# Feed-forward products by seven block products instead of eight, with tokens as the stationary operand

## The chip, the cores and the metric

The kernel runs on one core of one Trainium2 chip. The metric is the time of one execution on the device, in microseconds (us).

## The reference, cut to what matters

Two networks run one after the other on 256 tokens of width 1024: two layers with mixture-of-experts blocks, then two layers that each hold two gated feed-forward blocks of hidden width 2816. All data are float32. Only these four feed-forward blocks change:

```python
def _rmsnorm(x, g):
    xf = x.astype(jnp.float32)
    y = xf * lax.rsqrt(jnp.mean(xf * xf, axis=-1, keepdims=True) + NORM_EPS)
    return (y * g.astype(jnp.float32)).astype(x.dtype)

def _swiglu(x, w_in, w_out):
    gate, up = jnp.split(x @ w_in, 2, axis=-1)
    return (jax.nn.silu(gate) * up) @ w_out
...
        h = h + HALF * _swiglu(_rmsnorm(h, ffn1_norm[l]), ffn1_w_in[l], ffn1_w_out[l])
...
        h = h + HALF * _swiglu(_rmsnorm(h, ffn2_norm[l]), ffn2_w_in[l], ffn2_w_out[l])
```

## The kernel before

Activations lie turned: 128 features in the partitions, 256 tokens along the free dimension, so that the width of 1024 is eight chunks. Weights come by DMA, in tiles of 2 MB (`w_in`) and 1 MB (`w_out`), into a ring of six slots (`SLOTS`). SyncE issues the next tile of one fixed list when a slot comes free (`due`, `follow`, `refill`), always into the slot that was freed first.

`ffn_stage` is one feed-forward block in 11 steps of 256 hidden features. Both products hold a 128x128 piece of a weight as the stationary operand and move the 256 tokens past it. A step is 32 such matmuls for gate and up (`first_hidden` for step 0, L1450; `hidden`, L1465) and 16 for the product with `w_out` (`add`, L1476), which gathers in the four banks 0 to 3 over all steps. VectorE multiplies gate and up by the inverse RMS `r` (L1558, L1559), ScalarE applies silu (L1540), VectorE multiplies the two (L1562). `add` of a step runs on TensorE one step behind `hidden`, which is cover for this chain, except between step 0 and step 1: there `hidden` of step 1 waits for the last multiplication of step 0.

The inverse RMS comes from `vector_sum` (L334 to L336), a matmul with ones (`tensor_mean`, L342, put behind chunk 5 of step 0), `vector_turn` (L348, L349) and `scalar_root` (L355). The stage behind reads the sums out of the banks with `refresh` (L274) and multiplies by a gain with `gained` (L290). Two of the four blocks are `headed`: their input's squares were made in the stage ahead. The other two make them themselves.

In the trace, one float32 matmul of this program shows as two MATMUL and two LDWEIGHTS records; a transpose on TensorE (`pe.transpose`) shows as one of each.

## Time and profile before

| | |
|---|---|
| median of 3 runs | 2952.29 us (2952.22 to 2952.78) |
| the profiled execution: its span | 2949.0 us |
| outside the span, against the median | 3.3 us |
| TensorE busy | 2754.4 us, 93% of the span |
| VectorE busy | 744.4 us, 25% |
| ScalarE busy | 436.3 us, 15% |
| mean granted TensorE clock | 0.991 |
| the four feed-forward blocks, from the first matmul to that of the stage behind | 233.1, 231.5, 232.7 and 231.4 us |

The profile records one execution. The span runs from its first to its last instruction. The four blocks follow one another with a mixer stage between the two of each layer, and every stage waits for the one ahead.

### The profile page before, as it was taken

What the parts mean: (1) busy time and instruction counts of PE and PEld (TensorE: products, weight loads), DVE (VectorE), ACT (ScalarE), POOL (GpSimd) and SP (SyncE); (2) the same over time, 40 slices, a digit from 0 to 9 for tenths busy, and PEclk for the clock granted to TensorE, in tenths of its full rate; (3) what the DMA queues carried; (4) which work ended last, traced back from release to release, by engine and by line L of the source; (5) the groups of instructions that cost most, each with busy time, mean ns of one, the idle gap of its engine ahead of it and who ended that gap; (6) DMA issues with size and microseconds to landing.
All of it is one profiled execution on the core that took longest, in us unless ns stands there. A gap on an engine that the chain in (4) does not pass through costs nothing. (4 is left out here: it accounts for less than half of the span.)

```text
span 2949.0 us, 36516 instructions
## 1 busy us (share of the span) xinstructions
PE 2754.4 (93%) x16086; PEld 1897.0 (64%) x16086; DVE 744.4 (25%) x1552; ACT 436.3 (15%) x896; POOL 0.2 (0%) x4
## 2 busy tenths in 40 slices
PE   7999999888898998878999999999999999999998
PEld 3664433333666332223888888888888888788887
DVE  1242111111232110102111456411121143763111
ACT  2032111111322110001000312000010031221000
POOL 0000000000000000000000000000000000000000
PEclk9999999999999999999999999999999999999999
DMA  8334999999856999999345331234344453302340
GB/s 344 133 158 171 374 428 428 427 428 427 336 228 280 427 428 427 427 428 385 142 159 197 124 143 60 86 130 156 143 150 150 158 181 114 143 31 101 141 158 29
DMA packets 59384, 691.53 MB, mean 234 GB/s; under 512 B 10384, under 2 KB 13072, under 8 KB 14448
## 3 DMA queue, kind: packets, MB, share of 16 engines
q1 hardware_dynamic: 55408, 685.59, 57.9%
q10 hardware_dynamic: 3840, 3.93, 0.4%
q8 instruction: 109, 1.79, 0.3%
q14 instruction: 27, 0.22, 0.0%
HBM read 688.45 MB, written 1.05 MB: 234 GB/s over the span
## 5 line engine op out<-in xcount | busy, mean ns | idle before, releaser
L1465 PE MATMUL banks<-main,weight_ring 128*128 128x256 f32 x2560 | 559.4, 379 | 6.6 <-DVE main L1562 6.6
L1465 PEld LDWEIGHTS banks<-main,weight_ring 128*128 128x128 f32 x2560 | 486.1, 190 | 74.0 <-issue 8.1
L1154 PE MATMUL banks<-weight_ring,main 128*64 128x512 f32 (+1 forms) x1440 | 323.7, 595 | 28.9 <-DMA weight_ring<-in_gate_up 27.9
L1476 PE MATMUL banks<-main,weight_ring 128*128 128x256 f32 x1408 | 310.4, 379 | 0.0
L1476 PEld LDWEIGHTS banks<-main,weight_ring 128*128 128x128 f32 x1408 | 267.5, 190 | 36.4
L1674 PE MATMUL banks<-main,weight_ring 128*128 128x256 f32 x1248 | 275.3, 380 | 0.0
L1674 PEld LDWEIGHTS banks<-main,weight_ring 128*128 128x128 f32 x1248 | 236.5, 190 | 36.0 <-issue 4.5
L1154 PEld LDWEIGHTS banks<-weight_ring,main 128*64 128x64 f32 (+1 forms) x1440 | 90.5, 124 | 229.7 <-issue 182.4
L1558 DVE TENSOR_TENSOR main<-banks,tmp 128x256 f32<-128x256 f32 x88 | 37.3, 424 | 697.8 <-PE banks L1465 695.9
L1179 PE MATMUL banks<-weight_ring,main 128*64 128x512 f32 (+1 forms) x704 | 159.0, 595 | 37.1 <-DMA weight_ring<-in_down 36.7
L1282 DVE TENSOR_TENSOR main<-banks,main 64x512 f32<-64x512 f32 (+1 forms) x64 | 44.3, 692 | 482.5 <-ACT main L1248 482.5
L1540 ACT ACTIVATE main<-main 128x256 f32<-128x256 f32 x88 | 36.6, 416 | 773.5 <-DVE main L1558 773.5
L1179 PEld LDWEIGHTS banks<-weight_ring,main 128*64 128x64 f32 (+1 forms) x704 | 44.7, 124 | 148.9 <-issue 101.3
L1154 PE MATMUL banks<-main 128*32 128x512 f32 (+1 forms) x384 | 87.0, 595 | 10.3 <-DMA main<-in_gate_up 8.7
L1287 DVE COPY main<-banks 32x512 f32<-32x512 f32 x48 | 33.1, 690 | 244.7 <-PE banks L1179 244.2
L428 PE MATMUL banks<-main,weight_ring 128*128 128x512 f32 (+1 forms) x224 | 82.6, 527 | 6.3 <-ACT main L584 6.3
L1248 ACT ACTIVATE main<-banks 64x512 f32<-64x512 f32 (+1 forms) x64 | 37.5, 586 | 236.9 <-PE banks L1154 236.9
L428 PEld LDWEIGHTS banks<-main,weight_ring 128*128 128x128 f32 x224 | 44.2, 201 | 42.8 <-issue 36.9
L1893 DVE TENSOR_TENSOR main<-banks,tmp 128x256 f32<-128x256 f32 x86 | 35.7, 421 | 133.6 <-PE banks L1674 132.9
L1253 ACT ACTIVATE main<-banks 32x512 f32<-32x512 f32 x48 | 28.1, 586 | 266.1 <-PE banks L1179 265.8
L1450 PE MATMUL banks<-main,weight_ring 128*128 128x256 f32 x256 | 58.5, 388 | 7.4 <-DVE main L290 3.7
L1154 PEld LDWEIGHTS banks<-main 128*32 128x32 f32 (+1 forms) x384 | 22.9, 118 | 64.9 <-issue 49.3
(403 smaller groups left out, 2667.0 us busy)
## 6 DMA issues: line engine op xcount, KB each, us to landing
weight_ring<-in_gate_up SPq DMA_DIRECT2D x90, 2048.0 KB, 34.7
weight_ring<-in_f_in SPq DMA_DIRECT2D x44, 2048.0 KB, 7.7
weight_ring<-in_down SPq DMA_DIRECT2D x43, 2048.0 KB, 35.4
main<-in_gate_up SPq DMA_DIRECT2D x24, 2048.0 KB, 33.7
weight_ring<-in_mix_in SPq DMA_DIRECT2D x24, 2048.0 KB, 7.7
weight_ring<-in_ada_w SPq DMA_DIRECT2D x22, 2048.0 KB, 16.4
weight_ring<-in_f_out SPq DMA_DIRECT2D x44, 1024.0 KB, 4.8
constants<-in_gate_up SPq DMA_DIRECT2D x14, 2048.0 KB, 32.6
```

The costliest lines, as they stand in the source:

```text
L428: return pe.matmul(K.PS[:, c % BANKS, 0:m_], w[:, k, col * P:(col + 1) * P], H[:, k, 0:m_], start=k == 0, stop=k == KC - 1)
L1154: m = pe.matmul(K.PS[64 * j:64 * j + S * CAP, hf, :], x, w[:, k, j, :], start=kh + k == 0, stop=4 * kh + k == KC - 1, tile_position=(0, 64 ...
L1179: m = pe.matmul(K.PS[64 * j:64 * j + S * CAP, 3 + j, :], hT[:, k, 0:S * CAP], w[:, k % 4, j, :], start=k == 0, stop=k == KC - 1, tile_posi ...
L1248: K.mark(a_.activation(hs[64:64 + S * CAP, hf, :], K.PS[0:S * CAP, hf, :], ACT.Silu), K.act)
L1282: K.mark(v.tensor_tensor(hs[64:64 + S * CAP, hf, :], K.PS[64:64 + S * CAP, hf, :], hs[64:64 + S * CAP, hf, :], ALU.mult), K.dve)
L1450: m = pe.matmul(K.PS[:, 4 + c, g * SEQ:(g + 1) * SEQ], w[:, k, g, c * P:(c + 1) * P], H[:, k, :], start=g + k == 0, stop=g == 1 and k == K ...
L1465: m = pe.matmul(K.PS[:, 4 + c, g * SEQ:(g + 1) * SEQ], w[:, k, g, c * P:(c + 1) * P], H[:, k, :], start=g + k == 0, stop=g == 1 and k == K ...
L1476: m = pe.matmul(K.PS[:, o // 2, (o % 2) * SEQ:(o % 2 + 1) * SEQ], w[:, c, o * P:(o + 1) * P], hid[:, b, c, :], start=first and c == 0 and ...
L1540: a_.activation(sg[:, c, :], sg[:, c, :], ACT.Silu).then_inc(K.act.h, 1)
L1558: v.tensor_tensor(sg[:, c, :], K.PS[:, 4 + c, 0:SEQ], N.r, ALU.mult).then_inc(K.linear.h, 1)
L1674: m = pe.matmul(K.PS[:, bank(p), 0:SEQ], wt[:, k, (p % 4) * P:(p % 4 + 1) * P], H[:, k, :], start=k == 0, stop=k == KC - 1)
L1893: K.mark(v.tensor_tensor(Z[:, chunk, :], K.PS[:, bank(p), 0:SEQ], N.r, ALU.mult), K.read)
```

## The change

Gate and up. The normed tokens are made once (`Hn`, with `r` in them) and cut into a 2x2 grid: two halves of the 256 tokens (`t0`, `t1`) by two halves of the 1024 features. A weight tile is cut the same way, two halves of the features by two halves of its columns, each half holding 128 gate and 128 up columns (`ffn_tiles` lays it out so). Strassen's scheme (in Winograd's form) makes the four output blocks from seven block products in place of eight. Sums of token blocks (`S`) are made once per stage, differences of weight blocks (`mingle`) for every tile. In each block product the 128 tokens are stationary and 256 weight columns move, so the outputs come with tokens in the partitions. Step 0 stays as it was.

ScalarE copies four partial sums out of the banks in each step, VectorE adds three (`join`, `finish`), and both make the hidden values (`low`). These are turned back by four transposes a step (`turn`) and kept for all steps (`hid`).

The product with `w_out` now comes behind all gate products, no longer between them, again as seven products per 256 hidden features, each of them one matmul that moves 512 columns, summed over the 11 steps in seven banks. VectorE combines the banks, and 16 transposes turn the result (`turn_out`). The list of weight tiles follows the new order. `tensor_mean` stands behind chunk 2 (`headed`) or chunk 4. The loops are written out; before, they were hardware loops.

The diff, cut to its core (the old body of `ffn_stage`, which it removes, stands above):

```diff
         if self.source == "products":
-            p = K.PS[:, c // 2, (c % 2) * SEQ:(c % 2 + 1) * SEQ]
+            p = K.PS[:, 2 * (c // 4):2 * (c // 4) + 2, (c % 4) * P:(c % 4 + 1) * P]
+            x = x.rearrange("p (i t) -> p i t", i=TT)
...
-    MEAN = 6
+    n1 = n0 + STEPS
+    MEAN, TURNED, SIDE, OTHER = 6, 0, 2, 7
+    MEAN_AT = 2 if headed else 4
...
+            def product(out, a, t, b, begin, end):
+                for k in range(4):
+                    m = pe.matmul(out, a[:, k, t], b[:, k, :], start=begin and k == 0, stop=end and k == 3, skip_group_check=True)
+                return m
+            def turn(j):
+                pe.wait_ge(K.dve.h, hidden(j, 2))
+                if j > 1:
+                    pe.wait_ge(K.hread.h, K.hread.at(j - 1))
+                for place, i in enumerate((0, 2, 3, 1)):
+                    m = pe.transpose(K.PS[:, TURNED, place * P:(place + 1) * P], low[:, j % 2, i, :], K.ident)
+                K.mark(m, K.hturned)
+            def step(j):
+                n = n0 + j
+                b11, b12, b21, b22 = blocks(n)
+                T = B.T[:, j % 2]
...
+                if j == 1:
+                    pe.wait_ge(K.smade.h, K.smade.at(2))
+                if j > 2:
+                    pe.wait_ge(K.dve.h, hidden(j - 2, 2))
+                K.mark(product(main(j), Hn[:, 0:4], t0, b11, True, False), K.formed)
+                pe.wait_ge(K.mingled.h, weighed(n, 1))
+                if j == 1:
+                    pe.wait_ge(K.smade.h, K.smade.at(3))
+                else:
+                    pe.wait_ge(K.joined.h, joined(j - 1, 3))
+                K.mark(product(other(j), S[:, 2], t0, T[:, 0], True, False), K.formed)
+                if j > 1:
+                    turn(j - 1)
+                pe.wait_ge(K.mingled.h, weighed(n, 3))
+                if j == 1:
+                    pe.wait_ge(K.smade.h, K.smade.at(6))
+                pe.wait_ge(K.copied.h, copied(j, 1))
+                K.mark(product(main(j), S[:, 1], t0, T[:, 1], False, False), K.formed)
+                K.mark(product(side(j), Hn[:, 4:KC], t0, b21, True, True), K.formed)
+                pe.wait_ge(K.copied.h, copied(j, 3))
+                K.mark(product(main(j), S[:, 0], t0, b12, False, False), K.formed)
+                pe.wait_ge(K.mingled.h, weighed(n, 4))
+                K.mark(product(other(j), Hn[:, 4:KC], t1, T[:, 2], False, True), K.formed)
+                pe.wait_ge(K.copied.h, copied(j, 4))
+                K.mark(product(main(j), S[:, 3], t0, b22, False, True), K.used)
+            def add(u, i):
+                b11, b12, b21, b22 = rows(u)
+                T, n = B.TO[:, u % 3], n1 + u
+                if i == M1:
+                    K.arrived(pe, n)
...
+                    a, b = hid[:, 2 * u, t0], b11
+                elif i == M2:
+                    a, b = hid[:, 2 * u + 1, t0], b21
+                elif i == M6:
+                    pe.wait_ge(K.mingled.h, weighed(n, 4))
...
+                    a, b = sums(u, 1), T[:, 1, :]
...
+                    a, b = sums(u, 2), T[:, 0, :]
+                elif i == M4:
+                    a, b = hid[:, 2 * u + 1, t1], T[:, 2, :]
...
+                    a, b = sums(u, 0), b12
+                else:
+                    a, b = sums(u, 3), b22
+                return pe.matmul(K.PS[:, BANK[i], :], a, b, start=u == 0, stop=u == STEPS - 1, skip_group_check=True)
+            def turn_out(i, bank):
+                pe.wait_ge(K.banked.h, K.banked.at(i))
+                for c in range(4):
+                    m = pe.transpose(K.PS[:, bank, c * P:(c + 1) * P], ends[:, 2 + i, c * P:(c + 1) * P], K.ident)
+                K.mark(m, K.turned_out)
+            first_hidden()
+            for j in range(1, STEPS):
+                step(j)
+            for u in range(LATE):
+                for i in (M1, M2, M6, M7, M4, M5, M3):
+                    m = add(u, i)
+                K.mark(m, K.used)
+                if u == 0:
+                    turn(STEPS - 1)
+            for i in (M1, M2, M6, M7, M4, M5, M3):
+                for u in range(LATE, STEPS):
+                    m = add(u, i)
+                if i != M3:
+                    K.mark(m, K.summed_out)
+                if i == M7:
+                    pe.wait_ge(K.hread.h, K.hread.at(STEPS - 1))
+                    turn_out(1, 0)
+                if i == M5:
+                    turn_out(2, 1)
+            m.then_inc(K.used.h, 3)
+            K.used.count += 3
+            turn_out(3, 3)
+            turn_out(4, 2)
...
+            for j in range(1, STEPS):
+                if j > 1:
+                    a_.wait_ge(K.joined.h, joined(j - 1, 2))
+                copy(j, m1s, main(j), M1)
+                copy(j, m7s, other(j), M7)
+                if j > 1:
+                    a_.wait_ge(K.joined.h, joined(j - 1, 3))
+                copy(j, qs, main(j), M6)
+                if j > 1:
+                    read_turned(j - 1)
+                copy(j, q5s, main(j), M5)
+                if j == 1:
+                    for c in range(2):
+                        a_.wait_ge(K.linear.h, K.linear.at(2 * c + 1))
+                        K.mark(a_.activation(B.sg0[:, c, :], B.sg0[:, c, :], ACT.Silu), K.act)
+                a_.wait_ge(K.joined.h, joined(j, 3))
+                if j > 1:
+                    a_.wait_ge(K.dve.h, hidden(j - 1, 1))
+                K.mark(a_.activation(B.sg[:, 0:3, :], B.cs[:, :, t0], ACT.Silu), K.act)
+                a_.wait_ge(K.used.h, n0 + j + 1)
+                if j > 1:
+                    a_.wait_ge(K.dve.h, hidden(j - 1, 2))
+                K.mark(a_.activation(B.sg[:, 3, :], main(j)[:, t0], ACT.Silu), K.act)
...
+            def mingle_begin(n, parts, T):
+                b11, b12, b21, b22 = parts
+                K.arrived(v, n)
+                difference(T[:, 0], b22, b12)
+                difference(b12, b12, b11)
+            def mingle_end(n, parts, T):
+                b11, b12, b21, b22 = parts
+                settle()
+                difference(T[:, 1], b22, b12)
+                settle()
+                difference(T[:, 2], b21, T[:, 1])
...
+            def mingle(j):
+                parts = blocks(n0 + j), B.T[:, j % 2]
+                if j > 2:
+                    v.wait_ge(K.used.h, n0 + j - 1)
+                mingle_begin(n0 + j, *parts)
+                mingle_end(n0 + j, *parts)
...
+            def mingle_out(u):
+                parts = rows(u), B.TO[:, u % 3]
+                if u > 2:
+                    v.wait_ge(K.used.h, n1 + u - 2)
+                mingle_begin(n1 + u, *parts)
+                mingle_end(n1 + u, *parts)
...
+            def share(part, a, b):
+                pair = hid[:, 2 * a:2 * b, :].rearrange("p (u c) t -> p u c t", c=2)
+                a11, a12, a21, a22 = pair[:, :, 0, t0], pair[:, :, 1, t0], pair[:, :, 0, t1], pair[:, :, 1, t1]
+                out = B.shares[part]
+                K.mark(v.tensor_tensor(out[:, 0], a21, a22, ALU.add), K.shared)
+                K.mark(v.tensor_tensor(out[:, 2], a11, a21, ALU.subtract), K.shared)
+                v.wait_ge(K.shared.h, K.shared.at(4 * part + 1))
+                K.mark(v.tensor_tensor(out[:, 1], out[:, 0], a11, ALU.subtract), K.shared)
+                v.wait_ge(K.shared.h, K.shared.at(4 * part + 3))
+                K.mark(v.tensor_tensor(out[:, 3], a12, out[:, 1], ALU.subtract), K.shared)
...
+            def join(j):
+                v.wait_ge(K.formed.h, formed(j, M2))
+                v.wait_ge(K.copied.h, copied(j, 1))
+                if j > 1:
+                    v.wait_ge(K.dve.h, hidden(j - 1, 1))
+                K.mark(v.tensor_tensor(B.cs[:, 0, :], m1s, side(j), ALU.add), K.joined)
+            def finish(j):
+                v.wait_ge(K.copied.h, copied(j, 4))
+                K.mark(v.tensor_tensor(B.cs[:, 1, :], q5s, m7s, ALU.add), K.joined)
+                v.wait_ge(K.formed.h, formed(j, M4))
+                K.mark(v.tensor_tensor(B.cs[:, 2, :], qs, other(j), ALU.add), K.joined)
+                v.wait_ge(K.act.h, K.act.at(2 + 2 * (j - 1) + 1))
+                if j > 2:
+                    v.wait_ge(K.hturned.h, K.hturned.at(j - 2))
+                v.wait_ge(K.joined.h, joined(j, 3))
+                K.mark(v.tensor_tensor(low[:, j % 2, 0:3, :], B.cs[:, :, t1], B.sg[:, 0:3, :], ALU.mult), K.dve)
+                v.wait_ge(K.act.h, K.act.at(2 + 2 * (j - 1) + 2))
+                v.wait_ge(K.used.h, n0 + j + 1)
+                K.mark(v.tensor_tensor(low[:, j % 2, 3, :], main(j)[:, t1], B.sg[:, 3, :], ALU.mult), K.dve)
...
+            for b in range(2):
+                K.mark(v.tensor_tensor(Hn[:, 4 * b:4 * b + 4, :], H[:, 4 * b:4 * b + 4, :], bc(N.r, 1, 4), ALU.mult), K.smade)
+            v.wait_ge(K.smade.h, K.smade.at(2))
+            K.mark(v.tensor_tensor(S[:, 2], Hn[:, 0:4, t0], Hn[:, 0:4, t1], ALU.subtract), K.smade)
+            K.mark(v.tensor_tensor(S[:, 0], Hn[:, 0:4, t1], Hn[:, 4:KC, t1], ALU.add), K.smade)
+            v.wait_ge(K.smade.h, K.smade.at(4))
+            K.mark(v.tensor_tensor(S[:, 1], S[:, 0], Hn[:, 0:4, t0], ALU.subtract), K.smade)
+            v.wait_ge(K.smade.h, K.smade.at(5))
+            K.mark(v.tensor_tensor(S[:, 3], Hn[:, 4:KC, t0], S[:, 1], ALU.subtract), K.smade)
+            mingle_end(n0 + 1, *first)
+            gate_begin()
+            for j in range(1, STEPS):
+                if j > 1 and j + 1 < STEPS:
+                    mingle(j + 1)
+                if j == STEPS - 1:
+                    mingle_out(0)
+                    v.wait_ge(K.used.h, n0 + STEPS - 1)
+                    share(0, 0, 5)
+                join(j)
+                if j == 1:
+                    mingle(2)
+                    gate_end()
+                finish(j)
+            mingle_out(1)
+            v.wait_ge(K.used.h, n0 + STEPS)
+            v.wait_ge(K.hread.h, K.hread.at(STEPS - 1))
+            share(1, 5, STEPS)
+            for u in range(2, STEPS):
+                mingle_out(u)
+            m1, q, u3, c11, c21, c22, c12 = (ends[:, i, :] for i in range(7))
+            v.wait_ge(K.copied.h, K.copied.at(4 * (STEPS - 1) + 1))
+            v.wait_ge(K.summed_out.h, K.summed_out.at(2))
+            combine(c11, m1, K.PS[:, BANK[M2], :], K.banked)
+            v.wait_ge(K.summed_out.h, K.summed_out.at(3))
+            st(v.tensor_tensor(q, m1, K.PS[:, BANK[M6], :], ALU.add))
+            v.wait_ge(K.summed_out.h, K.summed_out.at(4))
+            st(v.tensor_tensor(u3, q, K.PS[:, BANK[M7], :], ALU.add))
+            v.wait_ge(K.summed_out.h, K.summed_out.at(5))
+            combine(c21, u3, K.PS[:, BANK[M4], :], K.banked)
+            v.wait_ge(K.summed_out.h, K.summed_out.at(6))
+            st(v.tensor_tensor(q, q, K.PS[:, BANK[M5], :], ALU.add))
+            combine(c22, u3, K.PS[:, BANK[M5], :], K.banked)
+            v.wait_ge(K.turned_out.h, K.turned_out.at(2))
+            following.vector_early(v)
+            v.wait_ge(K.used.h, n1 + STEPS)
+            combine(c12, q, K.PS[:, BANK[M3], :], K.banked)
+            if gains:
+                if loads:
+                    K.all_loaded(v)
+                following.vector_gained(v)
+            v.wait_ge(K.turned_out.h, K.turned_out.at(4))
...
-            for j in range(1, FC // 2):
-                t += [(TILE, win[layer, j]), (2 * D, wout[layer, j - 1])]
-            return t + [(2 * D, wout[layer, FC // 2 - 1])]
+            return [(TILE, win[layer, j]) for j in range(FC // 2)] + [(2 * D, wout[layer, j]) for j in range(FC // 2)]
```

## Rows read from the trace of the kernel before

**Rows 1.** Part 1 of the page: busy time and share of the engines.

```profile
PE 2754.4 (93%) x16086; PEld 1897.0 (64%) x16086; DVE 744.4 (25%) x1552; ACT 436.3 (15%) x896; POOL 0.2 (0%) x4
```

**Rows 2.** Busy time by stretch: the four blocks. Columns: stretch, length, engines, clock, DMA.

```profile
1382.90:1616.00 233.10, 230.50 (x1058) 202.01 (x1059) 33.85 (x84) 12.95 (x29) 0.00 (x0) 0.99 0.45 168
...
1923.80:2155.30 231.50, 228.84 (x1059) 200.90 (x1059) 32.28 (x77) 12.33 (x26) 0.00 (x0) 1.00 0.41 149
2155.30:2388.00 232.70, 230.10 (x1064) 202.00 (x1065) 36.65 (x92) 16.30 (x38) 0.00 (x0) 1.00 0.44 159
...
2704.70:2936.10 231.40, 228.78 (x1058) 200.78 (x1058) 31.96 (x76) 12.51 (x27) 0.00 (x0) 1.00 0.31 113
```

**Rows 3.** The same view: one step of the first block.

```profile
1435.32:1456.04 20.72, 20.72 (x98) 18.24 (x97) 2.36 (x6) 0.83 (x2) 0.00 (x0) 1.00 0.42 153
```

**Rows 4.** Timeline, start of the first block: start, length, engine and instruction, idle time before.

```profile
1382.89 12.29 PE L1450 MATMUL banks<-main,weight_ring 128*128 128x256 f32 x48 [3.68 <-DVE main L290]
...
1384.49 1.22 DVE L334 TENSOR_TENSOR main<-main 128x1024 f32<-128x1024 f32 x1
...
1395.01 0.59 PE L342 MATMUL banks<-tmp,constants 128*128 128x256 f32 x2
...
1395.44 3.62 PE L1450 MATMUL banks<-main,weight_ring 128*128 128x256 f32 x16
1395.64 0.42 DVE L348 TENSOR_SCALAR tmp<-banks 128x256 f32<-128x256 f32 x1 [8.74 <-PE banks L342]
...
1398.34 0.42 DVE L1558 TENSOR_TENSOR main<-banks,tmp 128x256 f32<-128x256 f32 x1 [0.48 <-ACT tmp L355]
...
1400.13 0.43 DVE L1562 TENSOR_TENSOR main<-main 128x256 f32<-128x256 f32 x1 [1.04 <-ACT main L1540]
...
1400.71 14.05 PE L1465 MATMUL banks<-main,weight_ring 128*128 128x256 f32 x64 [1.65 <-DVE main L1562]
```

**Rows 5.** Timeline of TensorE in the mixer: eight transposes (L1709) between matmuls.

```profile
1678.78 1.89 PE L1674 MATMUL banks<-main,weight_ring 128*128 128x256 f32 x8
1680.51 1.04 PE L1709 MATMUL banks<-constants,main 128*128 128x128 f32 x8
1681.38 0.81 PE L1674 MATMUL banks<-main,weight_ring 128*128 128x256 f32 x3
```

**Rows 6.** Groups by line: transposes of another stage. Busy us, mean ns of one.

```profile
L2151 PE MATMUL banks<-constants,main 128*128 128x128 f32 x64 | 8.2, 277 | 2.1 <-PEq L1628 2.1
```

**Rows 7.** Timeline of TensorE in the first network: matmuls that move 512 columns.

```profile
217.69 7.13 PE L962 MATMUL banks<-main,constants 128*128 128x512 f32 x16
224.66 0.60 PE L944 MATMUL banks<-constants,main 128*128 128x128 f32 x4
225.10 7.03 PE L962 MATMUL banks<-main,constants 128*128 128x512 f32 x16
231.97 0.60 PE L944 MATMUL banks<-constants,main 128*128 128x128 f32 x4
```

**Rows 8.** Groups by line, shapes apart: VectorE and ScalarE pieces of the size used.

```profile
L334 DVE TENSOR_TENSOR main<-main 128x1024 f32<-128x1024 f32 x6 | 7.3, 1224 | 1.1 <-PEq L2019 1.1
...
L858 ACT ACTIVATE main<-banks 128x512 f32<-128x512 f32 x16 | 9.6, 597 | 9.6 <-PE banks L759 9.5
...
L1540 ACT ACT_TABLE_LOAD x4 | 5.1, 1283 | 0.1
...
L858 ACT ACTIVATE main<-banks 128x256 f32<-128x256 f32 x8 | 3.1, 383 | 7.1 <-PE banks L759 7.1
```

**Rows 9.** Timeline of TensorE at the first block's end; L1662 is the mixer's.

```profile
1601.08 13.98 PE L1476 MATMUL banks<-main,weight_ring 128*128 128x256 f32 x64
1616.01 1.32 PE L1662 MATMUL banks<-main,weight_ring 128*128 128x256 f32 x5 [0.95 <-PEq L1440]
```

**Rows 10.** DMA issues of weights: KB each, median us from issue to landing.

```profile
weight_ring<-in_f_in SPq DMA_DIRECT2D x44, 2048.0 KB, 7.7
...
weight_ring<-in_f_out SPq DMA_DIRECT2D x44, 1024.0 KB, 4.8
```

More of the change, by code:

```diff
@@ L1425, with ffn_stage @@
 EXP_M_HALF = float(np.exp(-0.5))
[L1428 removed]
+def ffn_stage(K, N, B, headed, following, gains, loads=()):
     nc, n0, STEPS, H = K.nc, K.eaten, FC // 2, N.H
[L1433 to L1481 removed]
@@ new lines, in ffn_stage, with blocks @@
+    n1 = n0 + STEPS
+    MEAN, TURNED, SIDE, OTHER = 6, 0, 2, 7
+    MEAN_AT = 2 if headed else 4
+    M1, M7, M6, M2, M5, M4, M3 = range(7)
+    BANK = {M1: 4, M2: 5, M6: 6, M7: 7, M4: 1, M5: 3, M3: 2}
+    LATE = STEPS - 3
+    Hn, S, hid, low, ends = B.Hn, B.S, B.hid, B.low, B.ends
+    t0, t1 = slice(0, P), slice(P, 2 * P)
+    m1s, m7s, qs, q5s = (B.mid[:, i, :] for i in range(4))
+    def blocks(n):
+        w = K.slot(n).rearrange("p (k h f) -> p k h f", k=KC, h=2)
+        return w[:, 0:4, 0, :], w[:, 0:4, 1, :], w[:, 4:KC, 0, :], w[:, 4:KC, 1, :]
@@ new lines, in rows, with sums, main, other @@
+    def rows(u):
+        w = K.slot(n1 + u)[:, 0:2 * D].rearrange("p (c f) -> p c f", c=2)
+        return w[:, 0, 0:512], w[:, 0, 512:1024], w[:, 1, 0:512], w[:, 1, 512:1024]
+    def sums(u, i):
+        return B.shares[0][:, i, u, :] if u < 5 else B.shares[1][:, i, u - 5, :]
+    def main(j):
+        return K.PS[:, 1 if j % 2 else 3, 0:SEQ]
+    def other(j):
+        return K.PS[:, OTHER, 0:SEQ]
+    def side(j):
+        return K.PS[:, SIDE, 0:SEQ]
+    def formed(j, product):
+        return K.formed.at(6 * (j - 1) + product + 1)
@@ L1537, in silu, with first_hidden @@
-        def silu(a_, j):
-            for c in range(2):
-                a_.wait_ge(K.linear.h, 2 * j + K.linear.at(c + 1))
-                a_.activation(sg[:, c, :], sg[:, c, :], ACT.Silu).then_inc(K.act.h, 1)
+            def first_hidden():
+                K.arrived(pe, n0)
+                w = K.slot(n0).rearrange("p (k h g f) -> p k h g f", k=KC, h=2, g=2)
+                for k in range(KC):
+                    if not headed:
+                        pe.wait_ge(K.scaled.h, N.scaled_at(k))
+                    for c in range(2):
+                        for g in range(2):
+                            m = pe.matmul(K.PS[:, 4 + c, g * SEQ:(g + 1) * SEQ], w[:, k, c, g, :], H[:, k, :],
+                                          start=g + k == 0, stop=g == 1 and k == KC - 1, skip_group_check=True)
+                        if k == KC - 1:
+                            K.mark(m, K.used if c == 1 else K.pe)
+                    if k == MEAN_AT:
+                        N.tensor_mean(pe, MEAN)
@@ new lines, in gate_begin, with gate_end @@
+            def gate_begin():
+                for c in range(2):
+                    if c == 0:
+                        v.wait_ge(K.pe.h, K.pe.at(1))
+                    else:
+                        v.wait_ge(K.used.h, n0 + 1)
+                    K.mark(v.tensor_tensor(B.sg0[:, c, :], K.PS[:, 4 + c, 0:SEQ], N.r, ALU.mult), K.linear)
+                    K.mark(v.tensor_tensor(B.up0[:, c, :], K.PS[:, 4 + c, SEQ:2 * SEQ], N.r, ALU.mult), K.linear)
+            def gate_end():
+                for c in range(2):
+                    v.wait_ge(K.act.h, K.act.at(c + 1))
+                    v.wait_ge(K.linear.h, K.linear.at(2 * c + 2))
+                    K.mark(v.tensor_tensor(hid[:, c, :], B.up0[:, c, :], B.sg0[:, c, :], ALU.mult), K.dve)
@@ L1569, in _ @@
             N.vector_sum(v, st, here=not headed)
+            first = blocks(n0 + 1), B.T[:, 1]
+            mingle_begin(n0 + 1, *first)
             N.vector_turn(v, st, MEAN)
             N.ready(v)
-            gate(v, 0, 0)
-            gate(v, 1, 1)
-            with v.Fori(0, LOOPS) as i:
-                for b in range(BODY):
-                    gate(v, BODY * i + b + 2, (b + 2) % 3)
-            if loads:
-                K.all_loaded(v)
-            following.vector_early(v, gains)
-    K.pe.count += 2 * STEPS
```

198 lines of the change are left out of this document (73 added, 125 removed).

## The prediction

> **What bounds the kernel now.** I read the page's busy shares first: TensorE has 93% of the span, VectorE 25%, ScalarE 15% [rows 1]. Then the busy time by stretch, for the four feed-forward blocks: in 233.1 us TensorE is busy for 230.5, and the others look the same, at a granted clock of 0.99 to 1.00 and with the DMA engines at 0.31 to 0.45 [rows 2]. So TensorE's own pace sets these blocks. One step of 48 matmuls takes 20.72 us with TensorE busy throughout [rows 3]: 0.4317 us per float32 matmul of 256 columns. The weight loads are busy for 18.24 of the 20.72 us and lie beside the matmuls, so only moved columns count. VectorE works 2.36 us of a step. Last, the timeline: TensorE idles 1.65 us ahead of step 1, for the chain inverse RMS, silu, product [rows 4], and 0.95 us between two stages [rows 9].
>
> **Removed: matmuls.** Gate and up keep 32 matmuls in step 0 and go from 32 to 28 in each of 10 steps, all of 256 columns: 40 x 0.4317 = 17.3 us per block. The product with `w_out` goes from 176 matmuls of 256 columns (76.0 us) to 77 of 512. In the first network, eight of 512 columns take 224.66 - 217.69 = 6.97 us, and another eight 6.87 [rows 7]: 0.871 and 0.859 us each, against 0.863 for twice a 256-column one. I take 0.863, hence 66.5 us, 9.5 less; the two ends are 67.1 and 66.1.
>
> **Added on TensorE: transposes.** 4 for each of 10 steps and 16 at the end, 56 per block. Eight of them in the midst of matmuls like these take 1681.38 - 1680.51 = 0.87 us, and four take 225.10 - 224.66 = 0.44 [rows 5, 7], so 0.11 each: 6.2 us per block.  The other end is the recorded length of one, 0.277 [rows 6], if each had to wait for the one ahead; the rows show starts 0.11 apart, so I take 0.11.
> The Trainium skill ("TensorE: Matmul & The Clock Gate", Part 4: PE-mode transpose) puts a 128x128 transpose in a kernel's midst at about 275 ns. As a length that agrees with the 277 here. Were it the pace too, the four blocks would pay 61.6 us instead of 24.6; the starts in this trace speak against it.
>
> Steady work: 17.3 + 9.5 - 6.2 = 20.6 us less per block, 82.4 in all four.
>
> **A gate step in its new form.** TensorE needs 28 x 0.4317 + 0.44 = 12.5 us, seven products of 1.73. What it must wait for, with releases by [rows 4]: from a matmul to VectorE 0.2 us after TensorE's next instruction starts (1395.44 to 1395.64; I allow 0.3); from the end of a VectorE piece to TensorE 0.15 (1400.56 to 1400.71). A ScalarE copy of 256 columns is 0.38 us [rows 8]. So a copy's round trip is about 0.3 + 0.38 + 0.15 = 0.8 us. Each of the three that TensorE waits for (ahead of M6, M5 and M3) has one whole product of another bank as its cover, 1.73 us. `read_turned` (0.60) comes ahead of the copy behind M5, but is done by then: it starts after M6's copy and M2 and M5 run beside it. The sum `qs + other`, for which the next step's M7 waits, is made after M4 and has M3 and M1 as cover, 3.5 us. `turn` waits for silu and two products of the step before: ready about 1.2 us into the step, needed at 3.5. Were that cover gone, each copy would cost its round trip, 0.8 us.
> VectorE: four differences of 1024 elements at 1.22 [rows 8], three sums of 256 at 0.42, products of 384 and 128 (0.56 and 0.29, from 1.22 and 0.42 by 1.04 ns per element): 7.0 us of 12.5. It runs `mingle` from 1.2 to 6.2 us of the step and `join` is due at 7.6. ScalarE: four copies, one read of 0.60, silu of 384 and 128: 3.0 us, and two table loads of 1.28 [rows 8] at most if silu and copy should not share a table, which would lie where ScalarE waits.
>
> **Start of a block.** Now 1.65 us is lost ahead of step 1. `tensor_mean` moves up. In a `headed` block it is put behind 3 chunks, 5.2 us in, and r is ready 3.3 us later (1395.01 to 1398.34 in [rows 4]), at 8.5. Then VectorE makes `Hn` (two of 1.22), `S` (four of 0.69), two weight differences (1.22): the first product can start at 11.2, M6 at 15.3; TensorE comes at 14.3 and 17.7. No loss. (The first block's first 24 matmuls took 12.1 us, 1382.89 to 1395.01, where 24 x 0.4317 is 10.4, at a lower granted clock; step 0 stays, and so does that.) In the other two the mean is at 8.6, r at 12.0, `Hn` at 14.5, the third sum that M6 needs at 18.8 where TensorE comes at 18.0: 1.0 lost with the first wait. In all four, VectorE does `gate_begin`, `join`, `mingle(2)` (4.9) and `gate_end` in step 1, and its last sum is late for step 2's M7 by about 0.5. Against 4 x 1.65 = 6.6 lost now, that makes 2 x 1.0 + 4 x 0.5 = 4.0: 2.6 us less. What is late next is this VectorE queue in step 1.
>
> **From gate to output.** VectorE can make `share(1)` only when the last step is turned and read: 7.4 us into the output part, then 3.9 for it and 2.9 for `mingle_out(2)`, 14.2, where M6 of u = 2 comes at 14.25. I charge 0.15 per block, 0.6.
>
> **End of a block.** After M3, `c12` (0.69) waits until VectorE is through with four `refresh`; then `turn_out(4)`. From M3's end to the last transpose some 1.6 us, 0.9 of it counted as transposes above: 0.7 more per block, 2.8. The 0.95 between stages [rows 9] stays. The last stage has one `refresh` less to do, 0.4 back.
>
> **DMA.** A gate step asks for 2 MB in 12.5 us and an output step for 1 MB in 6.0; they land in 7.7 and 4.8 us, six slots ahead [rows 10]. The last three slots come free together at a block's end, but the mixer needs the fourth tile some 40 us later. SyncE's queue holds nothing else. I charge nothing.
>
> **Sum.** 82.4 + 2.6 - 0.6 - 2.8 + 0.4 = 82.0 us. The profiled span of 2949.0 becomes 2867.0; 3.3 us lie between it and the median of the runs, so 2870.3: **2870 us**.
>
> **Rivals.**
> 1. The seven products don't run through: one release per gate step is exposed, a copy's full round trip of 0.8 us in each of 40 steps, 32 us, 2902. For it: seven handovers a step where there were two, and three engines in one ring. Against: every cover above is at least twice its wait. 8%.
> 2. Transposes cost their length: 224 x (0.277 - 0.11) = 37 us, 2907. For it the length in [rows 6], against it the starts in [rows 5, 7]. 4%.
> 3. VectorE becomes the bound, and the kernel slower. From 7.0 us of work per step it would have to reach 12.5 to cost anything and 14.6 to eat the 82 us (2.05 us in each of 40 steps), from where on it is slower; at 15 us per step, 2970. The mechanism would be that pieces which read weights from the ring slow down beside TensorE and the DMA. Against: L334 took 1.22 us beside matmuls, the same as its mean [rows 4, 8]. 3%.
> That the kernel would not do what the change says I see no way for.
>
> **Range and chances.** The forecast has 83%. Its own range: low, 0.859 per 512 columns and the start and end losses gone, 2863; high, 0.871 to 0.88 (5 us), transposes at 0.13 (4 us), start and end losses doubled (7 us), 2886. The 80% range reaches somewhat into rival 1: 2862 to 2888. Beyond the low end 2% remain. Faster or slower by 0.2% (5.9 us) is about what a measurement of this kernel can tell from no change; rivals 1 and 2 are still faster, so faster 96%, same 1%, slower 3%.
>
> **What would show it.** Gate steps of 12.5 us with TensorE busy throughout and copies ended before their product's turn; an output step of 6.0; transposes 0.11 apart; blocks of some 211 us in place of 231 to 233, VectorE busy for more than half of each. Wrong if gate steps are longer than 13 us, if the profile names ScalarE or VectorE ahead of M6, M5 or M3, or if 512 columns cost more than 0.88.

## The result, and the profile after

The changed kernel takes 2865.6 us (median of 4 runs, 2862.0 to 2870.2), beside 2952.5 us for the kernel before (4 runs, 2952.2 to 2952.9): a ratio of 0.9703, with a 95% interval of 0.9692 to 0.9715, or 86.9 us less. Forecast were 2870 us and 82.0 us less.

The page of the changed kernel, part 1, answers to [rows 1]:

```profile
PE 2677.1 (93%) x15198; PEld 1711.8 (60%) x15198; DVE 1102.0 (38%) x1932; ACT 517.5 (18%) x1100; POOL 0.2 (0%) x4
```

TensorE keeps its share of 93%, now of a shorter span. It works 77 us less than before, VectorE 358 us more and ScalarE 81 us more, and nearly all of that extra work is hidden (the block starts below show what is not). The four blocks, cut from the first matmul of each to that of the stage behind (busy time by stretch, as [rows 2]):

```profile
1387.57:1598.99 211.42, 210.06 (x836) 154.66 (x837) 123.47 (x180) 33.26 (x80) 0.00 (x0) 0.99 0.45 167
1906.58:2115.62 209.04, 207.87 (x837) 153.64 (x837) 121.87 (x173) 32.58 (x77) 0.00 (x0) 1.00 0.40 147
2115.62:2325.35 209.73, 208.37 (x836) 153.47 (x837) 124.68 (x183) 35.20 (x85) 0.00 (x0) 1.00 0.45 166
2646.26:2855.52 209.26, 207.87 (x836) 153.61 (x836) 121.70 (x172) 32.86 (x78) 0.00 (x0) 1.00 0.31 115
```

They sum to 839.45 us. Before, cut in the same way, it was 233.12 + 231.43 + 231.43 + 231.47 = 927.45 us (the third stretch of [rows 2] reaches 1.3 us into the stage behind). So the blocks give 88.0 us. The rest of the program, which the change leaves alone, took 7.3 us more in this one profiled execution (2868.3 - 839.45 = 2028.85 against 2949.0 - 927.45 = 2021.55). Over the profiled executions of all kernels in this study it lies anywhere between 2021.5 and 2029.9, whatever was edited. Two stretches of the first network, before it reaches any changed code, show what differs. First the kernel before, then the changed one (75 to 100 and 150 to 175 us):

```profile
75.00:100.00 25.00, 25.00 (x119) 19.41 (x118) 2.63 (x5) 2.48 (x4) 0.00 (x0) 0.95 0.38 163
150.00:175.00 25.00, 24.28 (x148) 14.46 (x149) 11.65 (x32) 14.57 (x27) 0.00 (x0) 1.00 0.98 418
```

```profile
75.00:100.00 25.00, 25.00 (x111) 19.71 (x110) 2.66 (x5) 2.48 (x4) 0.00 (x0) 0.89 0.40 170
150.00:175.00 25.00, 24.10 (x141) 14.22 (x141) 10.85 (x30) 12.50 (x23) 0.00 (x0) 0.93 1.01 430
```

The third column from the end is the granted clock: 0.89 for 0.95 and 0.93 for 1.00, in code that is the same. The profiled execution was also the longest of the four. Hence the experiments below are read by the sum of the four blocks. Where an edit touches nothing, blocks 2 to 4 repeat to 0.01 us (the change against diff4late, below). Block 1 has one more source of change: its first 20 matmuls took 10.4 us in most profiled executions, at the lower clock for a part of them, and 8.7 us at full clock in exposed, diff4 and early. Those three sums are 1.7 us shorter for a reason that is not their edit.

One steady gate step (busy time by stretch, beside [rows 3]), then the joint between two steps in TensorE's timeline:

```profile
1457.46:1469.99 12.53, 12.53 (x62) 11.04 (x61) 6.84 (x10) 2.82 (x7) 0.00 (x0) 1.00 0.46 176
```

```profile
1430.68 1.89 PE L1515 MATMUL banks<-main,constants 128*128 128x256 f32 x8
...
1432.40 0.60 PE L1524 MATMUL banks<-constants,main 128*128 128x128 f32 x4
...
1432.84 0.38 PE L1515 MATMUL banks<-main,constants 128*128 128x256 f32 x1
```

A step lasts 12.53 us and TensorE is busy throughout, VectorE for 6.84 and ScalarE for 2.82 of it, where 12.5, 7.0 and 3.0 were forecast. Four transposes (L1524) take 1432.84 - 1432.40 = 0.44 us. The `w_in` and `w_out` tiles land 7.7 and 4.8 us after their issue, as in [rows 10].

The start of step 1 in the first block answers to [rows 4], the end of the block to [rows 9]. The timeline, all engines:

```profile
1401.29 2.36 DVE L1769 TENSOR_TENSOR main<-main,tmp 128x1024 f32<-128x1024 f32 x2 [0.48 <-ACT tmp L362]
...
1403.80 1.97 PE L1515 MATMUL banks<-weight_ring,main 128*128 128x256 f32 x8
...
1405.60 4.02 PE L1515 MATMUL banks<-main,constants 128*128 128x256 f32 x16
...
1407.61 1.23 DVE L1670 TENSOR_TENSOR main<-weight_ring,main 128x1024 f32<-128x1024 f32 x1
1407.62 1.59 PEld L1515 LDWEIGHTS banks<-main,constants 128*128 128x128 f32 x8 [0.54 <-DVE main L1670]
...
1417.52 0.41 DVE L1731 TENSOR_TENSOR constants<-constants,banks 128x256 f32<-128x256 f32 x1
...
1418.09 1.95 PE L1515 MATMUL banks<-main,constants 128*128 128x256 f32 x8
...
1596.57 0.60 PE L1593 MATMUL banks<-constants 128*128 128x128 f32 x4
1597.58 0.66 PE L1593 MATMUL banks<-constants 128*128 128x128 f32 x4 [0.41 <-DVE constants L1759]
1598.99 1.32 PE L1894 MATMUL banks<-main,weight_ring 128*128 128x256 f32 x5 [0.76 <-PEq L1488]
```

`Hn` (L1769) is ready 0.2 us after TensorE could have used it: the 12 matmuls from 1398.40 on end by their pace at 1403.58, and M1 starts at 1403.80. M7 and M6 of step 1 take 1409.45 - 1405.60 = 3.85 us where two products take 3.45: 0.4 us go where M6 waits for a weight difference (L1670). M7 of step 2 (1418.09) starts 0.16 us after the end of VectorE's last sum (L1731, 1417.93). The last four transposes wait 0.41 us for `c12` (L1759), and 0.76 us lie before the next stage.

What the start of a block costs is best read from a block's first matmul to a point where TensorE runs through again, less the matmuls between at 0.4317 us each. An idle time in the profile is shorter than this loss, since it counts from the modelled end of the last matmul, 0.16 us behind its place by the pace (a product of four matmuls shows 1.89 us, and the next starts 1.73 after it). Block 3 of the kernel before, then blocks 2 (`headed`) and 3 of the changed one, timeline of TensorE:

```profile
2155.28 10.60 PE L1450 MATMUL banks<-main,weight_ring 128*128 128x256 f32 x48 [0.95 <-PEq L1440]
...
2185.30 7.07 PE L1476 MATMUL banks<-main,weight_ring 128*128 128x256 f32 x32
```

```profile
1906.58 5.42 PE L1505 MATMUL banks<-main,weight_ring 128*128 128x256 f32 x24 [1.38 <-PEq L2251]
...
1936.50 0.60 PE L1524 MATMUL banks<-constants,main 128*128 128x128 f32 x4
...
2115.62 8.87 PE L1505 MATMUL banks<-main,weight_ring 128*128 128x256 f32 x40 [0.76 <-PEq L1488]
...
2146.24 0.60 PE L1524 MATMUL banks<-constants,main 128*128 128x128 f32 x4
```

Before, 65 matmuls, the mean's among them (28.06 us), take 30.02: 1.96 us lost. Now 69 matmuls (29.79 us) take 29.92 in block 2 and 30.62 in block 3: 0.13 and 0.83 us lost. The other two blocks agree, block 1 without the 1.7 us of lower clock that it has in both kernels.

### The profile page after: what moved, and what is told of

Its sections match the earlier page's. It is cut to its first block and busy times, and to the rows that moved or that the text cites. A ratio compares the mean times of both kernels' runs of the same rounds, so it can differ in the third digit from the quotient of the medians.

```text
span 2868.3 us, 35136 instructions
## 1 busy us (share of the span) xinstructions
PE 2677.1 (93%) x15198; PEld 1711.8 (60%) x15198; DVE 1102.0 (38%) x1932; ACT 517.5 (18%) x1100; POOL 0.2 (0%) x4
## 5 line engine op out<-in xcount | busy, mean ns | idle before, releaser
L1906 PE MATMUL banks<-main,weight_ring 128*128 128x256 f32 x1248 | 275.9, 381 | 0.0
L1906 PEld LDWEIGHTS banks<-main,weight_ring 128*128 128x128 f32 x1248 | 236.9, 191 | 36.1 <-issue 4.4
L1670 DVE TENSOR_TENSOR main<-weight_ring 128x1024 f32<-128x1024 f32 (+1 forms) x168 | 158.3, 942 | 67.0 <-PE banks L1587 64.2
L1587 PE MATMUL banks<-weight_ring,main 128*128 128x512 f32 x352 | 158.9, 592 | 0.0
L1515 PE MATMUL banks<-main,constants 128*128 128x256 f32 x640 | 151.4, 380 | 0.3
L1515 PE MATMUL banks<-weight_ring,main 128*128 128x256 f32 x640 | 151.3, 379 | 0.1
L1515 PE MATMUL banks<-weight_ring,constants 128*128 128x256 f32 x640 | 151.2, 379 | 0.0
L1515 PEld LDWEIGHTS banks<-weight_ring,main 128*128 128x128 f32 x640 | 121.4, 190 | 17.3 <-issue 0.9
L1515 PEld LDWEIGHTS banks<-weight_ring,constants 128*128 128x128 f32 x640 | 121.6, 190 | 16.5
L1515 PEld LDWEIGHTS banks<-main,constants 128*128 128x128 f32 x640 | 118.3, 190 | 16.2 <-DVE main L1670 1.1
L1587 PE MATMUL banks<-main 128*128 128x512 f32 x264 | 119.8, 592 | 0.0
L1587 PEld LDWEIGHTS banks<-weight_ring,main 128*128 128x128 f32 x352 | 66.3, 190 | 78.7 <-issue 78.4
L1161 PE MATMUL banks<-main 128*32 128x512 f32 (+1 forms) x384 | 86.9, 595 | 9.5 <-DMA main<-in_gate_up 7.9
```

The costliest lines, as they stand in the source:

```text
L1161: m = pe.matmul(K.PS[64 * j:64 * j + S * CAP, hf, :], x, w[:, k, j, :], start=kh + k == 0, stop=4 * kh + k == KC - 1, tile_position=(0, 64 ...
L1515: m = pe.matmul(out, a[:, k, t], b[:, k, :], start=begin and k == 0, stop=end and k == 3, skip_group_check=True)
L1587: return pe.matmul(K.PS[:, BANK[i], :], a, b, start=u == 0, stop=u == STEPS - 1, skip_group_check=True)
L1670: K.mark(v.tensor_tensor(out, a, b, ALU.subtract), K.mingled)
L1906: m = pe.matmul(K.PS[:, bank(p), 0:SEQ], wt[:, k, (p % 4) * P:(p % 4 + 1) * P], H[:, k, :], start=k == 0, stop=k == KC - 1)
```

## The experiments

Ten kernels ran. All but turns2, diff4, diff8 and diff4late do only work that the result needs; those four do some of it twice or more often, and nothing was left out of any. "Blocks" is the sum of the four block lengths in the profiled execution.

| kernel | time, us | blocks, us | against the change's 839.45 |
|---|---|---|---|
| before | 2952.5 | 927.45 | +88.0 |
| change | 2865.6 | 839.45 | |
| both8 | 2971.2 (4 runs) | 945.24 | +105.8 |
| gate8 | 2939.1 (1) | 907.49 | +68.0 |
| out8 | 2901.0 (1) | 877.21 | +37.8 |
| exposed | 2906.1 (1) | 878.10 | +38.7 |
| turns2 | 2893.9 (1) | 862.17 | +22.7 |
| mean5 | 2878.9 (1) | 847.76 | +8.3 |
| diff4 | 2893.1 (1) | 866.40 | +27.0 |
| diff8 | 3067.9 (1) | 1038.51 | +199.1 |
| early | 2868.9 (5) | 837.55 | -1.9 |
| diff4late | 2868.7 (4) | 839.48 | +0.0 |

**1. Eight products for seven: both8, gate8, out8.** The orientation, the order and the transposes stay as in the change; both parts, the gate products alone, or the output alone are made of eight plain block products, without weight differences, sums of token blocks and ScalarE's copies of partial sums; VectorE copies the finished banks.

```diff
-                K.mark(product(main(j), Hn[:, 0:4], t0, b11, True, False), K.formed)
...
-                K.mark(product(main(j), S[:, 3], t0, b22, False, True), K.used)
+                product(side(j), Hn[:, 0:4], t0, b11, True, False)
+                K.mark(product(side(j), Hn[:, 4:KC], t0, b21, False, True), K.formed)
...
+                product(main(j), Hn[:, 0:4], t0, b12, True, False)
+                K.mark(product(main(j), Hn[:, 4:KC], t0, b22, False, True), K.used)
```

> The new orientation alone: tokens stationary, weights moving, the same transposes and the same order of tiles, but eight block products in place of seven, in the gate steps 1 to 10 and in the output; no sums of tokens, no differences of weights, no partial sums (VectorE copies the finished banks). Theory (TensorE's moved columns set the blocks, all else is covered): 4 x 10 x 4 x 0.4317 = 69.1 us for the gate products and 4 x 11 x 0.859 = 37.8 for the output, less 1 to 2 us at the starts, over the changed kernel's 2865.6: 2971, so slower than the kernel before by some 19 us; blocks of about 235.5 us. Rival (part of the gain is the orientation, 512-column matmuls and fewer weight loads): no slower than 2952.

> Only the gate steps by eight products, tokens stationary, without weight differences, token sums and ScalarE copies; the output stays at seven. Theory: 69 us more, less about 1 us at the starts: blocks of 209.3 + 17 = 226.5 us, the whole 2934. Rival (the work that the seven products put on VectorE and ScalarE costs TensorE time): taking it away gives some back, blocks clearly under 225 us.

> Only the output by eight products of 512 columns, without differences, sums of hidden values and combined banks; the gate steps stay at seven. Theory: 11 matmuls of 0.859 us more per block, 9.4, less 0.2 where VectorE's queue at the seam is gone: blocks of 218.5 us, the whole 2903. Rival (covers at the seam or at the end cost more than seen): under 217 us.

both8 took 2971.2 us (2970.0 to 2973.5), a ratio to the kernel before of 1.0056 with an interval of 1.0039 to 1.0073: what the change brings beside the seventh product (the orientation with its transposes, the later output, the earlier mean) makes the kernel slower by 17.8 us in the blocks, or 0.6%. The 224 transposes at 0.11 us, 24.4 us, are more than all of it; the gains at the start and from 512 columns give a part back. One of its gate steps, by stretch:

```profile
1450.33:1464.58 14.25, 14.25 (x69) 12.55 (x68) 2.12 (x5) 1.40 (x3) 0.00 (x0) 1.00 0.40 147
```

14.25 us with TensorE busy throughout, against 12.52 or 12.53: the eighth product is 1.73 us, four matmuls of 0.4317. VectorE has 2.12 us of work here and 6.84 in the seven-product step, and TensorE's time differs by the product alone. Gate and output add up without remainder: 68.0 + 37.8 = 105.8. The output's 37.8 is 11 matmuls of 0.859 us in four blocks, to the tenth. The gate's 68.0 stands against 40 x 1.727 = 69.1: about 1.1 us is what the extra waits of the seven-product form cost in all, nearly all of it in blocks 1 and 3.

**2. One release exposed in each gate step: exposed.** M6 is issued ahead of M7, so that it no longer has a product between itself and the copy of M1 for which it waits.

```diff
-    M1, M7, M6, M2, M5, M4, M3 = range(7)
+    M1, M6, M7, M2, M5, M4, M3 = range(7)
```

> M6 straight behind M1 on the same bank, so that ScalarE's copy of M1 between them has no product as its cover; M7 and the transposes come behind M6, everything else as in the changed kernel. Theory: the round trip of release, copy and release shows in every gate step, 0.8 us x 40 = 32 us: steps of 13.3 us, the whole 2898. Rival (the copies are not on the path even so, since TensorE runs ahead through its queue): no change, steps of 12.5.

Two steps' joint in the timeline of TensorE:

```profile
1428.21 1.89 PE L1515 MATMUL banks<-weight_ring,main 128*128 128x256 f32 x8
1430.72 3.69 PE L1515 MATMUL banks<-main,constants 128*128 128x256 f32 x16 [0.63 <-ACT constants L1626]
1434.25 0.60 PE L1524 MATMUL banks<-constants,main 128*128 128x128 f32 x4
...
1441.60 1.89 PE L1515 MATMUL banks<-weight_ring,main 128*128 128x256 f32 x8
1444.11 3.69 PE L1515 MATMUL banks<-main,constants 128*128 128x256 f32 x16 [0.63 <-ACT constants L1626]
1447.64 0.60 PE L1524 MATMUL banks<-constants,main 128*128 128x128 f32 x4
```

M1 starts at 1428.21 and M6 at 1430.72, 2.51 us later where a product takes 1.73: 0.78 us of idle, the round trip that the prediction had put together from single releases as 0.8. The step is 1447.64 - 1434.25 = 13.39 us, 0.87 longer, since the two products behind the wait take 0.08 more as well. That is 35 us in 40 steps, where 32 were expected, and blocks 2 and 4 are 8.7 us longer each, ten times this. Blocks 1 and 3 have 2.6 and 2.9 us more, in step 1, where M6 now comes earlier than VectorE's differences: a wait of 1.86 us in each, and in block 1 a granted clock of 0.67 over the 5.24 us behind it. (The sum of 38.7 holds the 1.7 us by which the first matmuls of block 1 were faster here.) The cover is real: rival 1 describes the price rightly, and the order M1, M7, M6 is what avoids it.

**3. Every transpose twice: turns2.**

```diff
-                for place, i in enumerate((0, 2, 3, 1)):
+                for place, i in 2 * list(enumerate((0, 2, 3, 1))):
...
-                for c in range(4):
+                for c in 2 * list(range(4)):
```

> All transposes of hidden values and of the output are made twice into the same place, 224 more in all. Theory (they cost the distance of their starts, 0.11 us): 24.6 us more, 6.2 per block. Rival (they cost their recorded length of 0.273): 61 us more, 15.3 per block.

```profile
1430.78 1.89 PE L1515 MATMUL banks<-main,constants 128*128 128x256 f32 x8
1432.50 1.04 PE L1524 MATMUL banks<-constants,main 128*128 128x128 f32 x8
1433.38 1.89 PE L1515 MATMUL banks<-main,constants 128*128 128x256 f32 x8
```

224 more transposes cost 22.7 us, 0.10 each; eight of them take 1433.38 - 1432.50 = 0.88 us. At 0.109 each they would be 24.4; at each block's end the four that are added ahead of the last four fall into the wait for `c12`, which is gone from the list of waits here. In the changed kernel the recorded length of one is 273 ns on average (160 on L1524), so length and pace differ by a factor of 2.5, and rival 2 is out. The 275 ns that the Trainium skill ("TensorE: Matmul & The Clock Gate", Part 4: PE-mode transpose) gives for a transpose in a kernel's context, in a passage on bf16, agree with the length of these float32 ones and are not their price.

**4. A later mean: mean5.** `tensor_mean` stands behind chunk 5, as before the change.

```diff
-    MEAN_AT = 2 if headed else 4
+    MEAN_AT = 5
```

> The matmul of the mean square goes back behind chunk 5 of step 0, where it was before. Theory: the inverse RMS comes at 13.7 us, the first block product at 16.3 in place of 14.3, and M6 waits 0.6 more: 2.6 us lost ahead of M6 in each block against 0.2 (headed) and 0.6 (the others): 2.4 and 2.0 more per block, 8.8 in all. Rival (the first product only waits for the weights): no change.

TensorE waits 1.79 us for `Hn` (`PE banks L1515 <- DVE main L1769`, 7.1 us in 4 waits), and the blocks take 8.3 us more. Without the moved mean the change would have lost at a block's start what the kernel before lost there.

**5. VectorE loaded: diff4 and diff8.** In every `mingle` of a gate step, the last weight difference is made five or nine times in place of once, which adds 4 or 8 operations of 1.25 us.

```diff
-                difference(T[:, 2], b21, T[:, 1])
+                for _ in range(extra):
+                    difference(T[:, 2], b21, T[:, 1])
+                    settle()
+                difference(T[:, 2], b21, T[:, 1])
```

> The last weight difference of each gate tile from the second on is made five times over (the same values), 4 x 1.22 us more VectorE work in 9 gate steps of each block: 7.0 + 4.9 + settling = 12.1 us of the 12.52 that TensorE needs. Theory (covered as long as VectorE's step is shorter than TensorE's): 0 to 4 us more in all. Rival (every microsecond of VectorE work costs): 36 x 4.9 = 176 us more.

> The same with 8 more differences, 9.8 us more per gate step: VectorE needs about 17.0 us in a step. Theory: VectorE is now the bound and the step becomes its sum, 17.0 to 17.5 us in place of 12.52, 36 x 4.5 to 5.0 = 162 to 180 us more, 3028 to 3046; that is where the change would have been slower than the kernel before. Rival (something else is hidden in the step): steps well away from VectorE's sum.

diff8 was expected slower than the kernel before, and was: 3067.9 us. A step lasts 17.21 us and VectorE sets it. Busy time by stretch:

```profile
1478.57:1495.78 17.21, 14.44 (x60) 12.22 (x60) 16.27 (x19) 2.60 (x7) 0.00 (x0) 0.90 0.37 146
```

So the bound of rival 3 exists and lies where it was put: a gate step on VectorE that is longer than TensorE's 12.5 us. But the blocks' 199 us are more than the expected 162 to 180, and diff4, expected at 0 to 4 us, lost 27.0. The waits of TensorE in diff4 name the place:

```profile
PE banks L1518 <- DVE constants L1737: 19.5, 4, 4.9
```

and the timeline of TensorE and VectorE in its first block the time:

```profile
1409.98 6.27 DVE L1673 TENSOR_TENSOR main<-weight_ring,main 128x1024 f32<-128x1024 f32 x5
...
1417.17 0.41 DVE L1737 TENSOR_TENSOR constants<-constants,banks 128x256 f32<-128x256 f32 x1
...
1417.73 3.75 PE L1518 MATMUL banks<-main,constants 128*128 128x256 f32 x8 [4.86 <-DVE constants L1737]
1421.28 1.06 PE L1527 MATMUL banks<-constants,main 128*128 128x128 f32 x4
1422.13 2.28 PE L1518 MATMUL banks<-main,constants 128*128 128x256 f32 x8
```

Four waits of 4.9 us, one per block, all at M7 of step 2: in step 1 VectorE has `gate_begin` and `gate_end` beside the usual work, and five microseconds of added differences turn into 4.86 of waiting at once. By starts M7 comes 5.02 us late (1417.73 against 1410.98 + 1.73) for 5.0 us of added work, so nothing was free there. Behind the wait the clock is down: the product takes 3.55 us (1421.28 - 1417.73) at a granted clock of 0.50, the lower of the two levels, and the next is mixed (0.71 over the 9 us from 1417.73; the expectation for diff4late below says 0.67). That makes the wait cost 6.6 to 7.7 us per block, 28.7 in all, and the 27.0 are these less the 1.7 of block 1's faster first matmuls. It explains diff8 too: one first wait of 9.9 us per block, and eight later steps that are 4.7 us longer each (17.21 - 12.52), make 47.4 per block, and the clock behind the first wait the 2.4 that are left to 49.8.

**6. The same load, but not in step 1: diff4late.** To see whether that one place made all of diff4's loss, the four added differences begin in step 2.

```diff
-                mingle_end(n0 + j, *parts, extra=4)
+                mingle_end(n0 + j, *parts, extra=4 if j > 2 else 0)
```

> As diff4 (four superfluous differences of 1024 elements per gate step on VectorE), but not in the mingle that VectorE does in step 1; they begin with the one in step 2. In diff4 the trace shows TensorE waiting 4.86 us for VectorE ahead of M7 of step 2 and nowhere later, at a granted clock of 0.67 in the 9 us after it. My theory: that one place made all of diff4's 27 us, so here the four blocks sum to 839 to 843 (0 to +4) although VectorE is busy for nearly all of every later step. Rival: a VectorE that is nearly full costs TensorE something in every step (contention, or late releases too short to be listed); then the blocks keep 10 us or more of the 27.

The blocks sum to 839.48, the change's to within 0.03 us, and two steps of it show why, by stretch:

```profile
1445.47:1458.00 12.53, 12.53 (x62) 11.03 (x61) 11.73 (x14) 2.71 (x7) 0.00 (x0) 1.00 0.46 170
1458.00:1470.52 12.52, 12.52 (x61) 11.03 (x60) 11.72 (x14) 2.71 (x7) 0.00 (x0) 1.00 0.46 169
```

VectorE is busy for 11.7 of 12.5 us and TensorE does not notice. The whole loss of diff4 was one late sum per block, and nothing is paid here for a VectorE that reads and writes beside TensorE, 94% busy as it is.

**7. An attempt at a better version: early.** The two differences of the first tile are made ahead of the inverse RMS's chain on VectorE, so that M6 of step 1 finds them.

```diff
             mingle_begin(n0 + 1, *first)
+            mingle_end(n0 + 1, *first)
             N.vector_turn(v)
...
-            mingle_end(n0 + 1, *first)
             gate_begin()
```

> One change for the better: the two differences of the first tile (2.4 us of VectorE) are made while the inverse RMS is still on its way, so that M6 of step 1 no longer waits for the second of them (0.4 to 0.5 us in blocks 1 and 3), and the sixth sum is waited for only at M3. My theory: blocks 1 and 3 come out 0.4 to 0.6 us shorter, 2 and 4 unchanged (there the wait is for the sums), the four blocks sum to 838.5 in place of 839.5; no difference of the runs' times that can be measured (under 0.1%). Rival: VectorE's queue in step 1 was what held TensorE in blocks 2 and 4 too; then all four become shorter, by 2 us or more in all.

2868.9 us (2865.5 to 2870.5), a ratio to the kernel before of 0.9715 (0.9702 to 0.9728), which can't be told from the change's 0.9703. The block lengths say that it is a wash. M6's wait is gone in blocks 1 and 3 (M7 and M6 take 3.45 us for 3.85), but in block 3 the two differences delay the chain by more than that. Timeline of TensorE, block 3:

```profile
2126.92 1.97 PE L1515 MATMUL banks<-weight_ring,main 128*128 128x256 f32 x8 [0.63 <-DVE main L1772]
2128.72 3.62 PE L1515 MATMUL banks<-main,constants 128*128 128x256 f32 x16
```

Block 3 is 0.2 us longer (209.90 for 209.73), not 0.4 to 0.6 shorter as expected. Block 1 is 2.1 us shorter, but 1.7 of that lie in its first 20 matmuls, untouched by the edit, which ran here at full clock (8.87 us in the records, for 10.56 in the change's profile). Blocks 2 and 4 stay, so the rival is out too. Without block 1's 1.7 us early is 0.2 us shorter in the blocks, too little for the runs to show. None of the experiments beats the change by more.

## Why the prediction was right

**What it rested on.** TensorE's pace sets the blocks, so removed columns are removed time. That held: a product out of a gate step is 1.73 us of 14.25, and gate and output, measured apart, sum to what both8 takes more than the change.

**Step by step**, in us for all four blocks:

| step of the prediction | forecast | measured |
|---|---|---|
| gate products, 40 x 0.4317 per block | -69.2 | -69.1 (14.25 - 12.52 = 1.73 per step; gate8, with all waits: 68.0) |
| product with `w_out`, 77 matmuls of 512 columns | -38.0 (0.863 each) | -39.4 (0.859 each: eight in 1582.81 - 1575.94 = 6.87) |
| transposes | +24.6 (0.11 each) | +24.4 (1420.31 - 1419.88 = 0.436 for four in the records); turns2: 22.7 for as many again |
| start of the blocks | -2.6 (4.0 lost for 6.6) | -5.9 (1.9 lost for 7.8, by starts) |
| gate to output | +0.6 | 0 (no wait listed, and no loss by starts) |
| end of the blocks | +2.8 | +1.9 by starts: 0.57 added ahead of the last transposes in each, and between stages 0.97 for 1.12 in three blocks, 1.21 for 1.15 in the last |
| DMA, ScalarE, VectorE in steady steps | 0 | 0 (TensorE busy for 12.52 of 12.52) |
| sum of the blocks | -81.6 | -88.0 |

The measured terms add up to the 88.0 us within 0.1. In the blocks the forecast was 6.4 us short of what they gave: the pace of 512 columns accounts for 1.4 us, the transposes for 0.2, the start for 3.3, the seam from gate to output for 0.6 and the end for 0.9. For the run it was only 4.7 us too high, since the rest of the program took some 1.7 us more than reckoned (an estimate: medians less block sums); that much is chance. That the profiled execution took 2870.2 us, the forecast itself, is chance too: its rest of the program was 7.3 us longer. The 0.4 us that the prediction gives back in the last stage lies outside the blocks; from the last block's end to the span's, 12.78 us stand for 12.87. By its own terms the low end of its range is 2862 (2870.3 - 1.2 - 4.0 - 2.8), not 2863.

The start is the largest term, and it was missed on both sides. What was lost before was taken as the idle time of 1.65 us, where TensorE lost 1.96 by starts: 1.2 us for four blocks. What is lost now was sized too large, by 2.1 us. In the two blocks that are not `headed` the prediction expected 1.0 with the first wait, and 0.2 are lost ahead of M1, under 0.1 in it and 0.4 at M6. For all four it expected step 2's M7 to be 0.5 late, and it was on time, with 0.06 lost in it. The place was right (diff4 shows that VectorE's queue in step 1 has nothing to spare), the size was not. Lengths were added where starts lie closer: from `join` to the last sum, the lengths in the prediction make 0.42 + 4.9 + 0.84 + 0.42 + 0.42 = 7.0 us, and the trace has 1417.93 - 1411.38 = 6.55. That accounts for the 0.44.

**The rivals.** Rival 1, an exposed round trip: its price was right within a tenth (0.78 of idle, 0.87 with what follows), but all three copies were covered. Rival 2, transposes at their length: out by turns2. Rival 3, VectorE the bound: the mechanism is shown by diff8 and absent in the change, where VectorE works 6.84 of 12.53 us and 70% more than that (diff4late, 11.7) still costs nothing. The mechanism that the prediction gave for it, differences that slow down beside TensorE and the DMA, did not come: they took 1.22 us. A chance of 3% for it was fair for the steady step; the weak place was step 1, which the prediction had named as next to be late.

**What stays open.** The start, seam and end terms are read from single profiled executions and were not each isolated; only gate8, mean5, early, diff4 and diff4late bear on them. Of the 17.8 us that both8 loses to the kernel before, the parts (transposes, order of the output, place of the mean) are reckoned, not measured apart. Why the rest of the program varies by up to 8 us between executions was not tried. It shows in the granted clock of stretches with the same code, but what sets that clock from one execution to the next is not seen here.

## What to carry to other kernels

Where one engine is busy throughout, count what the change takes from it and adds to it at the pace of starts, not at the recorded length: that gave the steady part to a few per cent. Then look for the one step in which the helper engine has extra work. The slack of a steady step (here four added VectorE operations of 1.25 us, free) says nothing about the first step, where the same four cost 27 us. And an algorithm with fewer products can carry a layout that loses by itself: the layout with its transposes cost 17.8 us, seven products for eight gave 105.8.

## What was unexpected of the hardware

A short wait costs more than its length, when the clock falls with it. After 4.86 us of idle in diff4 four matmuls took 3.55 us in place of 1.73, at a granted clock of 0.50. Shorter waits go either way. The first line is of mean5, the second of exposed, the last two of diff8, each from TensorE's timeline:

```profile
1404.63 1.97 PE L1515 MATMUL banks<-weight_ring,main 128*128 128x256 f32 x8 [1.79 <-DVE main L1769]
...
1402.48 5.41 PE L1515 MATMUL banks<-main,constants 128*128 128x256 f32 x16 [1.86 <-DVE main L1671]
...
1444.70 1.97 PE L1518 MATMUL banks<-main,constants 128*128 128x256 f32 x8 [1.93 <-DVE constants L1737]
...
1479.13 2.52 PE L1518 MATMUL banks<-main,constants 128*128 128x256 f32 x8 [2.07 <-DVE constants L1737]
```

After 1.79 us (mean5) the clock stayed at 1.00 and nothing more was lost. After 1.86 us (exposed) it averaged 0.67 over 5.24 us, where two products take 3.45. After 1.93 us (diff8) it stayed at 1.00 again. After 2.07 us (diff8) four matmuls took 2.30 us, the clock at 0.78. So a shorter idle time cost 1.8 us beyond itself and a longer one nothing: the length of the idle stretch alone does not tell what follows.
